# A gMLP mixer inside a four-layer trunk: v projected in token order, LayerNorm along the free axis, plain fp32 mixing placed between the projection units of u

## What is computed

```python
def gmlp_mixer(h, w_in, ln_g, ln_b, w_s, b_s, w_out):   # h: (1, 512, 1024)
    uv = jax.nn.gelu(h @ w_in)                          # w_in: (1024, 4096)
    u, v = jnp.split(uv, 2, axis=-1)                    # each (1, 512, 2048)
    v = layer_norm(v, ln_g, ln_b)
    v = v.reshape(B, S // 128, 128, 8, 256)             # 4 chunks of 128 tokens, 8 groups
    w_mix = jnp.where(causal, w_s, 0.0)                 # (8, 128, 128)
    v = jnp.einsum('gts,bnsgc->bntgc', w_mix, v) + b_s.T[:, :, None]
    return (u * v.reshape(B, S, 2048)) @ w_out
```

## Time and profile before

| | |
|---|---|
| timed runs, median (lowest to highest) | 3128.26 us (3127.31 to 3128.5) |
| span of the profiled execution | 3131.6 us |
| PE busy, share of the span | 3017.3 us, 96% |
| DVE / ACT / POOL busy | 1427.0 / 1024.5 / 604.1 us |
| mean granted TensorE clock | 0.960 of full speed |

### The profile page before, as it was taken

The page is one execution under the profiler, slowest core; times in us unless marked ns, Lnnn a source line. Parts: engine busy times, 40 slices in busy tenths (PEclk is TensorE's granted clock), DMA queues, the critical chain, the costliest instruction groups (busy, mean ns, idle before and its releaser), DMA issues.

```text
span 3131.6 us, 39645 instructions
## 1 busy us (share of the span) xinstructions
PE 3017.3 (96%) x14948; PEld 2509.6 (80%) x14948; DVE 1427.0 (46%) x1851; ACT 1024.5 (33%) x1639; POOL 604.1 (19%) x447
## 2 busy tenths in 40 slices
PE   7989999999979999999999998999999998999998
PEld 6878888887778878888887776788888887888887
DVE  4455443336433555433354555353333556353333
ACT  4344332223412334322232223243223434242222
POOL 1225022202100001222012211112210225212210
PEclk9989999999965799999999999999999998999999
DMA  4322233333210002333332221323333330323331
GB/s 125 107 73 61 67 108 100 96 96 94 81 61 1 1 1 62 107 100 92 99 108 74 76 72 54 94 75 100 95 98 91 106 94 28 101 78 102 93 93 64
DMA packets 481908, 252.89 MB, mean 81 GB/s; under 512 B 8833, under 2 KB 479601, under 8 KB 481665
## 3 DMA queue, kind: packets, MB, share of 16 engines
q1 hardware_dynamic: 475904, 242.31, 26.7%
q10 hardware_dynamic: 5280, 6.82, 0.7%
q0 software_dynamic: 608, 2.16, 0.2%
HBM read 248.11 MB, written 2.10 MB: 80 GB/s over the span
## 4 chain that ended last, share of the span: by engine, by line
PE 89%; DVE 4%; issue 3%; POOL 2%; ACT 2%; DMA 0%; SPq 0%; POOLq 0%; ACTq 0%; DVEq 0%
PE acc L435 24%; PE acc L437 24%; PE acc L436 24%; PE acc L776 3%; PE tr L764 1%; PE acc L454 1%; PE acc L851 1%; PE acc L450 1%; PE acc L451 1%; PE st L752 1%; PE acc L752 1%; DVE work L1309 1%; PE acc L724 1%; POOL SS L1745 1%; DVE w_lo L1247 1%
## 5 line engine op out<-in xcount | busy, mean ns | idle before, releaser
L1247 DVE TENSOR_TENSOR w_lo<-w_raw,w_hi 128x1024 fp32r<-128x1024 f32 x461 | 629.8, 1368 | 923.6 <-ACT w_hi L915 923.5
L435 PE MATMUL acc<-a_hi,w_hi 128*128 128x512 f32 x2344 | 925.0, 395 | 6.4 <-DVE y_lo L1681 5.1
L437 PE MATMUL acc<-a_hi,w_lo 128*128 128x512 f32 x2344 | 913.6, 390 | 0.0
L436 PE MATMUL acc<-a_lo,w_hi 128*128 128x512 f32 x2280 | 888.1, 390 | 0.0
L915 ACT ACTIVATE w_hi<-w_raw 128x1024 fp32r<-128x1024 f32 x461 | 483.2, 1050 | 415.9 <-PE acc L437 410.9
L435 PEld LDWEIGHTS acc<-a_hi,w_hi 128*128 128x128 f32 x2344 | 441.1, 188 | 105.4 <-issue 16.5
L437 PEld LDWEIGHTS acc<-a_hi,w_lo 128*128 128x128 f32 x2344 | 440.8, 188 | 92.1
L436 PEld LDWEIGHTS acc<-a_lo,w_hi 128*128 128x128 f32 x2280 | 428.4, 188 | 91.0 <-issue 4.3
L437 PE MATMUL acc<-hid_hi,w_lo 128*128 128x512 f32 (+1 forms) x704 | 264.7, 376 | 0.0
L435 PE MATMUL acc<-hid_hi,w_hi 128*128 128x512 f32 (+1 forms) x704 | 264.7, 376 | 0.0
L436 PE MATMUL acc<-hid_lo,w_hi 128*128 128x512 f32 (+1 forms) x704 | 264.7, 376 | 0.0
(11 more groups left out here) (297 smaller groups left out, 3872.7 us busy)
## 6 DMA issues: line engine op xcount, KB each, us to landing
w_raw<-ffn_w_gate SPq DMA_DIRECT2D x88, 512.0 KB, 3.7
w_raw<-ffn_w_up SPq DMA_DIRECT2D x88, 512.0 KB, 3.7
w_raw<-gm_w_in SPq DMA_DIRECT2D x64, 512.0 KB, 4.1
w_raw<-ffn_w_down SPq DMA_DIRECT2D x64, 512.0 KB, 3.8
w_raw<-ret_w_in SPq DMA_DIRECT2D x48, 512.0 KB, 3.8
w_raw<-gm_w_out SPq DMA_DIRECT2D x32, 512.0 KB, 3.9
w_raw<-ffn_w_down SPq DMA_DIRECT2D x32, 384.0 KB, 3.3
w_raw<-nsa_w_in SPq DMA_DIRECT2D x21, 512.0 KB, 3.8
```

What stands on the lines that cost most here:

```text
L435: pe.matmul(o_bank, lhs_hi, rhs_hi, start=start, stop=False)
L436: pe.matmul(o_bank, lhs_hi, rhs_lo, start=False, stop=False)
L437: return pe.matmul(o_bank, lhs_lo, rhs_hi, start=False, stop=stop)
L1247: dve.tensor_tensor(w_lo[:, slot, :, :], w_raw[:, slot, :, :], w_hi[:, slot, :, :].bitcast(f32), ALU.subtract).then_inc(lo_done, 1)
```

## The change

**v in token order.** w_in's v half is loaded in blocks of 256 rows by 512 columns (the same 512 KB), and the roles in the matmul are swapped: 128 tokens of `a_hi` or `a_lo` are stationary, 512 columns of weights move. A value group `grp` (4 of them) gives v for 4 x 128 tokens by 512 features in the four banks; it takes four blocks kq, each with 24 matmuls. ACT applies gelu straight from PSUM with the RMS factor `r4` as scale per partition and writes `gvt`. The first group is `value_entry`: token tiles 0 and 1 in the first half, tile 2 in the second, tile 3 after it.

**LayerNorm along the free axis.** The DVE takes `bn_stats` of each 128x512 piece of `gvt` and `bn_aggr` of each token tile, ACT the root of a 128x4 tile, the DVE its reciprocal, and four passes `(v - mean) * rstd` over 128x2048. Both POOL sums, the centring, the squares, the two `ones` matmuls over `SS` and the transposes of v are gone. Gain and bias are applied after the mixing: two plain fp32 matmuls of 512 columns with `ones` give the row sums of the masked, transposed `ws` (`ws_sum`), and the bias goes in as `ws_sum * ln_b + b_s`.

**Plain fp32 mixing between the u units.** Tile m is mixed by four plain fp32 matmuls, 128 channels of `gvt` stationary and 128 columns of `ws_t` moving, into `tr`. It is issued behind u unit m + 2 (`MIX_LAG`); tiles 14 and 15 are mixed between the first pieces of the output projection. The DVE forms the gate (`gate_in`), POOL multiplies by u only, ACT rounds, and `g_lo` is the DVE's work now (`low_part`). Of the output projection, the loop over m holds the 16 pieces of the first output tile (before: 24).

The diff, cut to its core:

```diff
-                    stream(L["n_in"], 4, 4, gm_in(GM_WIDTH), ONE, first)
...
+                        sp.dma_start(wide(w_raw, n % SLOTS),
+                                     gm_w_in[z, 2 * P * kq:2 * P * (kq + 1), GM_WIDTH + VAL_W * grp:GM_WIDTH + VAL_W * (grp + 1)]
+                                     .rearrange("(k p) m -> p k m", p=P)).then_inc(loaded[n % SLOTS], 16)
...
+                    tiles = (0, 1) if hf == 0 else (2,)
+                    for k in range(DT):
+                        if hf == 0 and k % 2 == 0:
+                            pe.wait_ge(lo_done, n0 + k // 2 + 1)
+                        pe.wait_ge(a_hi_done, step_of(b, hf, k))
+                        for c in tiles:
+                            piece_of(c, k, w_hi, a_hi, k == 0, False)
+                            piece_of(c, k, w_lo, a_hi, False, False)
+                        pe.wait_ge(a_lo_done, step_of(b, hf, k))
+                        for c in tiles:
+                            last = piece_of(c, k, w_hi, a_lo, False, k == DT - 1)
...
-                            last = product(acc[:, mix_bank(L, m), c * P:(c + 1) * P], vt_hi[:, m % 2, c, :], vt_lo[:, m % 2, c, :],
-                                           ws_hi[:, m // 2, :], ws_lo[:, m // 2, :], True, True)
...
+                            if kq == 0:
+                                pe.wait_ge(gelu_done, 2 * M * z + 4 * (grp - 1) + c + 1)
+                            for kk in range(2):
+                                k, at_c = 2 * kq + kk, slice(c * P, (c + 1) * P)
+                                last = product(acc[:, (o0 + c) % BANKS, :], a_hi[:, k, at_c], a_lo[:, k, at_c],
+                                               wide(w_hi, n % SLOTS)[:, kk, :], wide(w_lo, n % SLOTS)[:, kk, :], k == 0, k == DT - 1)
...
+                        for g2 in range(2):
+                            last = pe.matmul(st[:, g2, :], ones[:, :], ws_t[:, 4 * g2:4 * g2 + 4, :], start=True, stop=True)
...
+                def mix(m):
+                    if m == 0:
+                        pe.wait_ge(vn_done, CH * (z + 1))
+                    wait(pe, xb_done, M * z + m - 1 if m >= 2 else 0)
+                    for c in range(CH):
+                        last = pe.matmul(tr[:, m % 2, c * P:(c + 1) * P], gvt[:, c, m * P:(m + 1) * P], ws_t[:, m // 2, :], start=True, stop=True)
+                    last.then_inc(mix_done, 1)
+                for j in range(M):
+                    n = n0 + 16 + j
+                    pe.wait_ge(lo_done, n + 1)
+                    if j < BANKS:
+                        pe.wait_ge(gelu_done, 2 * M * z + 12 + j + 1)
+                    else:
+                        pe.wait_ge(acc_free, o0 + j - BANKS + 1)
+                    for k in range(DT):
+                        last = product(acc[:, (o0 + j) % BANKS, :], w_hi[:, n % SLOTS, k, :], w_lo[:, n % SLOTS, k, :],
+                                       a_hi[:, k, :], a_lo[:, k, :], k == 0, k == DT - 1)
+                    last.then_inc(unit_done, 1)
+                    if j >= MIX_LAG:
+                        mix(j - MIX_LAG)
+                for m in range(M):
+                    pe.wait_ge(g_lo_done, M * z + m + 1)
+                    piece(L["n_out"], L["o_out"], 2, m // KMAX, m % KMAX, g_hi, g_lo)
+                    if m == 2:
+                        mix(M - 2)
+                    if m == 5:
+                        mix(M - 1)
...
-                    dense(L["n_in"], L["o_in"], 4, 4, ONE, a_hi, a_lo, entry_of=L["b_in"])
...
+                    gmlp(L)
+                    dense(L["n_out"], L["o_out"], 2, 8, TWO, g_hi, g_lo, begun=2, tail_of=L["b_mid"])
...
+                    for j in range(M):
+                        split_unit(n0 + 16 + j + AHEAD)
+                        if j == 0:
+                            act.wait_ge(var_rd, z + 1)
+                            act.activation(vsd[:, :], vsd[:, :], ACT.Sqrt).then_inc(var_root, 1)
+                        act.wait_ge(acc_free, o0 + j + 1)
+                        act.activation(gu[:, j, :], gu[:, j, :], ACT.Gelu_apprx_tanh).then_inc(gelu_done, 1)
+                        if 0 <= j - MIX_LAG - 1 < M // 2:
+                            high(j - MIX_LAG - 1)
+                    act.wait_ge(unit_done, n0 + 2 * M)
+                    for m in range(M // 2, M):
+                        high(m)
...
+                        dve.bn_stats(vstat[:, c, grp, :], gvt[:, c, VAL_W * grp:VAL_W * (grp + 1)]).then_inc(v_stat, 1)
...
+                    def gate_in(m):
+                        dve.scalar_tensor_tensor(work[:, m % 2, 0:P], ws_sum[:, m // 2, :], lnp[:, 32 + M * z + m:33 + M * z + m],
+                                                 bs[:, m // 2, :], ALU.mult, ALU.add).then_inc(bt_done, 1)
+                        dve.wait_ge(mix_done, M * z + m + 1)
+                        dve.wait_ge(bt_done, M * z + m + 1)
+                        wait(dve, pm_done, M * z + m - 2 if m >= 3 else 0)
+                        dve.scalar_tensor_tensor(work[:, 2 + m % 3, :].rearrange("p (c t) -> p c t", c=CH),
+                                                 tr[:, m % 2, :].rearrange("p (c t) -> p c t", c=CH), lnp[:, M * z + m:M * z + m + 1],
+                                                 work[:, m % 2, 0:P].unsqueeze(1).broadcast_to([P, CH, P]),
+                                                 ALU.mult, ALU.add).then_inc(xb_done, 1)
+                    for j in range(M):
+                        split_unit(n0 + 16 + j + AHEAD)
+                        if j == 0:
+                            dve.wait_ge(var_root, z + 1)
+                            dve.reciprocal(vsd[:, :], vsd[:, :]).then_inc(rstd_ready, 1)
+                            dve.wait_ge(r_ready, L["b_in"] + 1)
+                            dve.wait_ge(rstd_ready, z + 1)
+                            for c in range(2):
+                                dve.tensor_scalar(gvt[:, c, :], gvt[:, c, :], vmv[:, c, 0:1], vsd[:, c:c + 1], ALU.subtract, ALU.mult).then_inc(vn_done, 1)
+                        leave(n0 + 16 + j, gu[:, j, :], (o0 + j) % BANKS, R[:, :])
+                        if j == 0:
+                            for c in range(2, CH):
+                                dve.tensor_scalar(gvt[:, c, :], gvt[:, c, :], vmv[:, c, 0:1], vsd[:, c:c + 1], ALU.subtract, ALU.mult).then_inc(vn_done, 1)
+                        if j == MIX_LAG:
+                            dve.wait_ge(bs_in, 16 * (z + 1))
+                            dve.wait_ge(ws_sum_done, z + 1)
+                        if j >= MIX_LAG:
+                            gate_in(j - MIX_LAG)
+                        if j >= MIX_LAG + 2 and j - MIX_LAG - 2 < M // 2:
+                            low_part(j - MIX_LAG - 2)
+                    gate_in(M - 2)
+                    for m in range(M // 2, M - 1):
+                        if m == M // 2 + 2:
+                            gate_in(M - 1)
+                        low_part(m)
+                    low_part(M - 1)
...
-                        m = k - 1
-                        if m >= 0:
-                            pool.wait_ge(g_hi_done, M * z + m + 1)
-                            pool.tensor_tensor(g_lo[:, m, :], work[:, 2 + m % 3, :], g_hi[:, m, :].bitcast(f32),
-                                               ALU.subtract).then_inc(g_lo_done, 1)
+                    for m in range(M):
+                        pool.wait_ge(gelu_done, 2 * M * z + M + m + 1)
+                        pool.wait_ge(xb_done, M * z + m + 1)
+                        pool.tensor_tensor(gu[:, m, :], work[:, 2 + m % 3, :], gu[:, m, :], ALU.mult).then_inc(pm_done, 1)
```

More of the change, by code:

```diff
@@ L39 @@
 GM_GROUPS = 8
+VAL_GROUPS = 4
+VAL_W = GM_WIDTH // VAL_GROUPS
+MIX_LAG = 2
 H_NSA = 16
@@ L473, in entry @@
                     if k == 1:
-                        pe.wait_ge(h_part, b + 1)
-                        for c in range(CH):
-                            total = pe.matmul(tr[:, 1, CH + c:CH + c + 1], work[:, 2, c * P:(c + 1) * P], ones[:, 0:1], start=True, stop=True)
-                        total.then_inc(stat_r, 1)
+                        h_total(b)
                     if k == 4:
-                        pe.wait_ge(r4_ready, 3 * b + 1)
-                        for c in range(CH):
-                            spread = pe.transpose(st[:, 1, c * P:(c + 1) * P], r4[:, c:c + 1].broadcast_to([P, P]), ident[:, :])
@@ new lines, in h_total, with h_spread @@
+            def h_total(b):
+                pe.wait_ge(h_part, b + 1)
+                for c in range(CH):
+                    total = pe.matmul(tr[:, 1, CH + c:CH + c + 1], work[:, 2, c * P:(c + 1) * P], ones[:, 0:1], start=True, stop=True)
+                total.then_inc(stat_r, 1)
+            def h_spread(b):
+                pe.wait_ge(r4_ready, 3 * b + 1)
+                for c in range(CH):
+                    spread = pe.transpose(st[:, 1, c * P:(c + 1) * P], r4[:, c:c + 1].broadcast_to([P, P]), ident[:, :])
+                spread.then_inc(r_spread, 1)
@@ L556, in piece @@
```

(7 more changed lines are left out.)

317 lines of the change are left out of this document (132 added, 185 removed).

## The result

The changed kernel took 3054.2 us (median of 4 runs, 3053.39 to 3059.05) against 3128.38 us before (4 runs, 3127.31 to 3130.23). The ratio is 0.9753, with a 95% interval of 0.9741 to 0.9765: 74.2 us less. The profiled execution took 3059.05 us, its span is 3057.3 us; the two profiled spans differ by 74.3 us.

What follows compares the result with a forecast made beforehand. PE bounds the kernel, losing time to LayerNorm's detour and the low clock after it. Replacing 79.0 and 76.3 us by 24.3, less 15.7 of shift, saves 39.0 and 36.3, 75.3 in all: 3053.0 us, range 3043 to 3073.

Steps and rivals of the forecast that it cites:

- v projection at 5.44 a block, its load covered: v phase: 16 blocks of 24 matmuls stay at 5.44 us each; loads land in 4.1 us, so PE never waits.
- Entry -1.0: Entry to the v phase: 72 matmuls of 512 columns replace 144 of 256, 1.0 us less per layer; bounds 0 and -2.
- First gelu +1.2: Start of v: PE waits for gelu, behind R's copy and a table load, to free bank 0; +1.2 us, bounds 0 and 3.
- Transposes 1.0, row sums 1.8, mean -0.9: ws transposes and row sums move into the v phase, +1.0 and +1.8 us; the mean's matmul leaves the u phase, -0.9.
- 14 mixing tiles of 0.97 between the u units: u phase: plain fp32 mixing costs PE 0.97 us a tile, between 0.89 and 1.13; 14 tiles add 13.6 us per layer.
- The shift of E, +15.7: End of the last u unit comes 15.7 us later per layer, from entry, gelu, transposes, row sums, mean and mixing.
- 24.3 behind E: After the last u unit: two mixing tiles, 32 output pieces and 0.6 for the square take 24.3 us, replacing 79.0 or 76.3.
- Normalisation 3 us early: DVE between v's last gelu and the first mixing: statistics and four passes of 2.2 us end 3 us before they are needed.
- late normalisation: Rival: slower DVE passes delay the first mixing some 5 us a layer; with the tail 14 us lost, 3067; 0.09 with late tail.
- four loads per matmul: Rival: each fp32 mixing matmul's four passes cost like separate matmuls, 0.44 us, 1.78 a tile; +26 us, 3079; chance 0.04.
- the fall of the clock in the u phase: Rival: short mixing matmuls bring PE to 1.2 GHz, 78 us more per layer, 3209; 0.03, shared with other causes over 70 us.
- the 57 us of overhead per layer: Kernel before, layer 0, last u bank to second output tile: 57 of 79.0 us are LayerNorm, transposes and mixing; 54 in layer 3.

Runs made afterwards that it cites:

- experiment 6: Changed kernel with gelu's table loaded early, first two gelus ahead of R's copy, row sums of ws by reduction and transposes: 3055.9 us beside 3061.4 for the changed kernel.
- experiment 3: Changed kernel with all 16 mixing tiles behind the u units instead of between them, output pieces four tiles behind: 3096.2 us.
- those four kernels: Kernel before, 3128.38 us; the same with useless matmuls filling PE's idle stretches further, 3122.1; changed with mixing behind the u units, 3096.2; changed, 3054.2.

## Why the prediction was right

3053.0 us was forecast and 3054.2 measured, 75.3 us to be saved and 74.2 saved. The mechanism held: of the signs that it named, the distance behind E came out at 25.6 us (24.5) with one wait of 0.17, and the u banks 6.35 apart (6.4) at a clock of 1.00. But several terms were off and cancel, so that the sum is closer than its terms.

- *v projection at 5.44 a block, its load covered*: right. PE waits nowhere in it but at the first gelus, and the load lands in 4.1 us.
- *Entry -1.0*: wrong in size. From the first scaling to R's copy layer 3 takes 33.14 us instead of 33.88, 0.74 less; in layer 0, from the first rounding of the activations, 28.26 (21.84 to 50.10) instead of 28.15, nothing.
- *First gelu +1.2*: right, 1.2 in both layers, of which a wait of 0.69 costs 0.94 (experiment 6).
- *Transposes 1.0, row sums 1.8, mean -0.9*: measured at PE's starts, 0.88 (74.97 to 76.08, less one step of 0.227), 1.71 and 0.91.
- *14 mixing tiles of 0.97 between the u units*: wrong twice. A tile costs 0.91, close to the lower bound of 0.89; plain fp32 matmuls have the 0.11 of a short fp32r record, twice, not the 0.12 of the longer one. And 13 tiles stand ahead of E, not 14: `mix(13)` is issued behind unit 15. 13 x 0.91 = 11.8 in place of 13.6. The prediction's own timetable of the tail, with tile 14 mixed by E+4.0, had all three tiles behind E; the sum had two.
- *The shift of E, +15.7*: the entry's -1.0 in it lies ahead of R's copy, so from there the forecast is 16.7. It was 14.7: 11.8 + 1.2 + 0.9 + 1.7 - 0.9.
- *24.3 behind E*: it was 25.6, for the same miscount. Three tiles follow E, 3 x 0.91 = 2.7, with 21.8 for the pieces, 0.6 for the square, and one wait for `g_lo` named 0.17 that cost 0.43: 25.5. I had put that wait at 0 and the low parts at 0.7; ACT and POOL kept pace, and a low part beside POOL's product took up to 1.8, the same turn-taking as in experiment 3. The bound of 2 us covered it.
- *Normalisation 3 us early*: it was 6.8 early, mostly because a pass over 2048 elements takes 1.34 us, not 2.2.

What cancels: 16 tiles priced 0.06 too high are 1.0 us a layer, 1.9 in all. Against them stand the entry, which gained 0.6 us over both layers in place of 2.0, and the wait for `g_lo`, 0.9. That these offset each other is luck; so is the last part of the agreement of the times, since layers that the change doesn't touch differed by 2.4 us, and the same kernel gave 3061.4 on another chip.

The rows of the mixing, of the low parts on tiles 8 to 15, and of the normalisation, in groups by line over the whole span after:

```profile
L704 PE MATMUL tr<-ws_t,gvt 128*128 128x128 f32 x256 | 33.7, 274 | 0.0
...
L1638 DVE TENSOR_TENSOR g_lo<-gu,a_hi 128x512 fp32r<-128x512 f32 x16 | 14.3, 953 | 0.0
...
L1661 DVE TENSOR_SCALAR gvt<-gvt,vmv,vsd 128x2048 f32<-128x2048 f32 x4 | 5.2, 1343 | 0.2
```

PE waited 0.0 us for the 128 mixing matmuls. The low parts took 953 ns on average, between my 0.7 and the bound of 1.05.

Of the rivals, late normalisation would have needed another 6.8 us on DVE; four loads per matmul are excluded by 0.2225 a matmul; and the fall of the clock in the u phase by the eightfold mixing at 1.00. The rule that speaks against the change was the Trainium skill's (FP8 and Floating Point Precision, TensorE Precision Notes), four passes for true fp32. The trace fits its count: 0.2225 us are close to 4 x 128 columns at 2.4 GHz (0.213). It is yet no argument, because the three fp32r products that such a matmul replaces took 3 x 0.11 = 0.33.

Where the 57 us of overhead per layer that the prediction named went can now be split. In layer 0, 38.7 us were saved: 8.1 were the low clock, 10.5 the new arithmetic (LayerNorm out of the way, one pass on POOL in place of two, no transposes of v, fewer matmuls, less what it adds in the v phase), 20.1 the place between the u units. In layer 3: 5.2, 10.8 and 20.1. The split is by those four kernels in that order; the one with the mixing behind had a stretch of low clock of its own at its end (0.53 from 248 to 254 us, 0.85 from 254 to 258), so some 3 us of the 20.1 may be clock.

## What to carry to other kernels

A side chain that makes TensorE wait is well put between units of dense work on it: here it then cost only its own matmuls, and the place was worth twice what the new arithmetic was. Before summing such a change, count which instances fall on either side of the mark that you measure at; my miscount moved 0.9 us from one term to another and was harmless only because both counted. And where DVE and POOL both read SBUF, price a short DVE instruction by what POOL is doing at that moment, not by its size.
